# Two layers on one core: the sum of squares of the attention output one weight unit later, and another order behind it on ScalarE and VectorE

## The reference

```python
qkv = xn @ w_qkv                                 # 2048 -> 3 * 2048, weights in fp32
q = rotary(rmsnorm(q, q_g)); k = rotary(rmsnorm(k, k_g))      # 8 heads of 2 x 128
p = softmax(masked(q k^T * scale))               # per head two maps of 256 x 256, in blocks of 128
w = p[:, :, 0] - lam * p[:, :, 1]
o = w @ v                                        # 256 features per head
o = rmsnorm(o, subln_g) * (1.0 - lambda_init)    # over the 256 features of one head
h = h + o.reshape(b, s, 2048) @ w_o
```

## Time and profile before

| | us |
|---|---|
| median of 3 executions | 2826.38 |
| lowest and highest | 2822.13, 2827.9 |
| the profiled execution | 2824.52 |
| its span, first to last instruction | 2822.7 |
| TensorE busy | 2742.0 (97%) |
| VectorE busy | 1984.2 (70%) |
| ScalarE busy | 1192.2 (42%) |
| granted TensorE clock, mean | 0.99 |

### The profile page before, as it was taken

One profiled execution on the slowest core, in us unless ns is written; L12 is line 12 of the kernel. 1 busy time (PEld: TensorE's weight loads), 2 busy tenths in 40 slices (PEclk: granted clock), 3 DMA queues, 4 the chain that ended last, 5 costly groups with the idle time before them and its releaser, 6 DMA issues.

```text
span 2822.7 us, 43966 instructions
## 1 busy us (share of the span) xinstructions
PE 2742.0 (97%) x15236; PEld 2383.8 (84%) x15236; DVE 1984.2 (70%) x2617; ACT 1192.2 (42%) x1517; POOL 5.7 (0%) x12
## 2 busy tenths in 40 slices
PE   6899999999999999999999999999999999999999
PEld 5787888877877888888888888888888888888888
DVE  6555477776767777766777776687777776677765
ACT  2102454444444444444444543355444444444443
POOL 0000000000000000000000000000000000000000
PEclk9999999999999999999999999999999999999999
DMA  9886655544444666666666566654466666666664
GB/s 299 292 259 202 206 188 179 182 142 153 153 131 155 189 192 186 186 191 188 192 187 188 184 200 189 187 162 133 141 193 182 189 193 190 187 192 186 191 199 146
DMA packets 705761, 528.13 MB, mean 187 GB/s; under 512 B 32205, under 2 KB 694543, under 8 KB 705423
## 3 DMA queue, kind: packets, MB, share of 16 engines
q1 hardware_dynamic: 701728, 523.60, 60.6%
q10 hardware_dynamic: 3951, 3.44, 0.4%
HBM read 523.80 MB, written 2.10 MB: 186 GB/s over the span
## 4 chain that ended last, share of the span: by engine, by line
PE 88%; DVE 6%; issue 2%; DMA 2%; ACT 2%; ACTq 1%; SPq 0%; DVEq 0%
PE acc L647 75%; PE acc L727 2%; PE acc L715 2%; PE acc L916 2%; PE turned L727 1%; PE sums L727 1%; DVE wr L1653 1%; DVE pro_ada L1728 1%; DMA aring<-in_w_ada 1%; DMA two_qturn<-two_q 1%; ACT wr L1204 1%; PE sums L655 0%; PE mixed L837 0%; PE sums L1031 0%; ACTq L1235 0%
## 5 line engine op out<-in xcount | busy, mean ns | idle before, releaser
L647 PE MATMUL acc<-xs,wr 128*128 128x512 f32 (+1 forms) x7680 | 1351.1, 337 | 0.2 <-DVE wr L1653 0.2
L647 PEld LDWEIGHTS acc<-xs,wr 128*128 128x128 f32 x7680 | 1174.9, 188 | 163.6 <-issue 3.8
L1653 DVE TENSOR_TENSOR wr<-raw,wr 128x1024 fp32r<-128x1024 f32 x832 | 1002.0, 1222 | 374.6 <-ACT wr L1204 360.7
L1204 ACT ACTIVATE wr<-raw 128x1024 fp32r<-128x1024 f32 x832 | 870.7, 1058 | 799.0 <-PE acc L647 784.7
L647 PE MATMUL acc<-ys,wr 128*128 128x512 f32 (+1 forms) x4352 | 766.2, 338 | 6.5 <-DVE ys L1687 6.5
L647 PEld LDWEIGHTS acc<-ys,wr 128*128 128x128 f32 x4352 | 669.8, 189 | 98.2 <-DVE ys L1687 6.4
L647 PE MATMUL acc<-wr,xs 128*128 128x512 f32 (+1 forms) x1024 | 193.5, 348 | 0.0
L647 PEld LDWEIGHTS acc<-wr,xs 128*128 128x128 f32 x1024 | 163.6, 195 | 24.3 <-issue 0.5
L1546 ACT ACTIVATE ffn_cv<-ffn_cv 128x256 f32<-128x256 f32 x88 | 36.9, 419 | 245.3 <-DVE ffn_cv L2234 245.3
L1664 DVE TENSOR_REDUCE ffn_ug<-acc 128x512 f32<-128x1024 f32 x88 | 107.8, 1225 | 39.6 <-PE acc L647 39.6
L1728 DVE SCALAR_TENSOR_TENSOR pro_ada<-aring,small,pro_ada 128x512 f32<-128x512 f32 (+1 forms) x112 | 92.4, 825 | 31.3 <-DMA aring<-in_w_ada 24.7
(11 more groups left out here) (306 smaller groups left out, 1504.8 us busy)
## 6 DMA issues: line engine op xcount, KB each, us to landing
raw<-in_ffn_w_up SPq DMA_DIRECT2D x704, 256.0 KB
raw<-in_ffn_w_down SPq DMA_DIRECT2D x160, 512.0 KB
raw<-in_a_w_qkv SPq DMA_DIRECT2D x96, 512.0 KB
raw<-in_b_w_kv SPq DMA_DIRECT2D x64, 512.0 KB
aring<-in_w_ada SPq DMA_DIRECT2D x96, 256.0 KB, 6.6
w<-in_w_in SPq DMA_DIRECT2D x48, 512.0 KB
raw<-in_w_ada SPq DMA_DIRECT2D x32, 512.0 KB, 6.1
raw<-in_w_out SPq DMA_DIRECT2D x32, 512.0 KB
```

Source lines behind the costliest of these rows:

```text
L647: mm = pe.matmul(*ops, start=first and ops is wide, stop=last and ops is wide)
L1204: f(wr[:, s, :, 0:256], raw[:, s, :].rearrange("p (k n) -> p k n", k=UK), ACT.Copy)\
L1653: tt(wr[:, s, :, 256:512], raw[:, s, :].rearrange("p (k n) -> p k n", k=UK), wr[:, s, :, 0:256], ALU.subtract).then_inc(T.unit_split[s].se ...
```

## The change

TensorE calls `diff_out_sums` behind unit 3 of the v pair, not behind unit 2. ScalarE issues the exchange DMAs of q behind the first of two units and not behind the second, and those of k ahead of the output's squares and not behind them. VectorE turns k and splits one more unit between the addition of the squares and the wait for their roots, and makes the low half of `ys` (now `diff_out_lo`) behind the evacuation of v. The last head calls the same two functions one behind the other, in the order that it had.

```diff
 in_v (TensorE)
-                        if live and n == 2:
+                        if live and n == 3:
                             diff_out_sums()
 two_heads (ScalarE)
-                    hi(2)
+                    hi(1)
                     turn_copy(qturn, qA, 1)
+                    hi(1)
                     act.wait_ge(*T.acc_read.next())
                     squares_of(S[1], 1)
                     hi(1)
                     root(2 * TOK, HD)
+                    turn_copy(kturn, kA, 2)
+                    T.heads_out.n += 1
                     if live:
                         diff_out_squares()
-                    turn_copy(kturn, kA, 2)
-                    T.heads_out.n += 1
                     hi(2)
 diff_out (VectorE)
-            def diff_out(tiles, turn=None):
+            def diff_out(turn=None):
...
                 tt(sq[0][:, 0, :], sq[0][:, 0, :], sq[0][:, 1, :], ALU.add).then_inc(*T.out_squares.one())
+                if turn:
+                    turn()
+                    split_units(1)
                 dve.wait_ge(*T.rs_ready.next())
                 for d in range(2):
                     w = stt(tmp[0][:, d, :], oA[:, d, :], small[:, 40 + d:41 + d], rs[:, 0, :], ALU.mult, ALU.mult)
                 w.then_inc(*T.split_me.one())
-                if turn:
-                    turn()
+
+            def diff_out_lo(tiles):
                 own(T.split_me)
                 lo(ys[:, tiles, :], tmp[0][:, :, :])
 two_heads (VectorE)
                     if live:
-                        diff_out(slice(0, 2) if first else bass.ds(i * 4 + (2 + 2 * e), 2), lambda: head_turn(kA, kturn))
+                        diff_out(lambda: head_turn(kA, kturn))
                     else:
                         T.sq_ready.n += 2
                         head_turn(kA, kturn)
-                    split_units(1 if live else 2)
+                        split_units(2)
                     evac(vA[:, :, :], by="partitions")
+                    if live:
+                        diff_out_lo(slice(0, 2) if first else bass.ds(i * 4 + (2 + 2 * e), 2))
 behind the loop (VectorE)
-            diff_out(slice(14, 16))
+            diff_out()
+            diff_out_lo(slice(14, 16))
```

## The result

The changed kernel takes 2792.7 us, the median of four executions (2792.3 to 2795.6), against 2827.1 before. The ratio is 0.9883, with a 95% interval of 0.9866 to 0.9900 (the quotient of the two medians, 0.9878, lies in it too). The profiled executions, 2824.52 and 2792.86, are 31.7 us apart where the sum said 25.4. One execution further down, of the kernel with the TensorE edit alone, took 3840.8 us at a granted clock of 0.66; its ratio leaves that one out, and the median without it is 2811.5 in place of 2811.6.

The account below looks back on a forecast made before the run. TensorE, busy 97% of the span, was taken as the bound, so only its pauses or slow stretches could pay. Terms -16.85, -7.6 and -1.0 gave -25.4 us, from 2824.52 to 2799.1, stated as 2800, range 2794 to 2810.

Parts of the forecast that it names:

- the sum: Total saving over the two-heads code and the last head: 25.4 us off the profiled 2824.52 us.
- The wait at L1044: TensorE's idle time before the squares' product, in seven heads, goes: -16.85 us.
- This edit alone takes the whole wait: Issuing product L1044 one unit later on TensorE removes its wait by itself: at least -16.7 us over seven heads.
- the reorderings do not take the wait; they give it a margin: ScalarE's and VectorE's new orders only make the squares' addition ready earlier, 2.1 us ahead of V3's end.
- The clock: Half-clock dips behind five of the seven L1044 pauses vanish with the pauses: -7.6 us, bounds 0 and -10.9.
- rival A: The clock is not given back after the pauses go: gain 17.8 us, 2807.6 us; chance 0.08.
- The last head: Behind the loop, the second scores product's 0.98 us wait for ScalarE's exponentials goes: -1.0 us, bounds 0 and -1.0.
- bare work: Distance between neighbouring L1044 rows less the wait: one head without pause or dip, 39.95 us.
- The walk: Step-by-step timing of the second head under the new order, from the trace of before; product L1044 starts at 615.75.
- B: The stall moves to the scores bank, TensorE waiting 1 us a head: 2814.6 us; chance 0.05.
- C: k's exchange DMAs land late and hold up VectorE's turn of k: slower, 2834 us; chance 0.03.
- D: Nothing changes because the waits at L1044 only stand one unit later: 2826 us; chance 0.03.

Follow-up runs that it names:

- orders-only kernel: The changed kernel with the product L1044 back behind unit 2, so only ScalarE's and VectorE's new orders remain: 2801.0 us, ratio 0.9913.
- five copies: The changed kernel with five 128x512 copies added on VectorE between v's evacuation and the low part of ys, in each of seven heads: 2803.3 us, ratio 0.9925.
- k's DMAs late: The changed kernel with k's exchange DMAs issued behind the roots of the output, about 9 us later: 2825.2 us, ratio 1.0003.

## Why the prediction was right, and where not

*The wait at L1044* (-16.85): right in sum and in place; no idle time in any of the seven heads, and the addition ends some 2 us ahead of the product, as said.

*"This edit alone takes the whole wait"; "the reorderings do not take the wait; they give it a margin"*: the step that failed. I looked at what L1044 waits for and not at who waits for L1044. Moving the product by 2.8 us moves the roots, and in the old order VectorE turned k behind them: 1.1 us a head at the first scores product, in seven heads of seven. The edit alone gives 13.8 us (2825.5 to 2811.6), the whole change 34.4; of the stage, 13.7 and 27.5. VectorE's new order, costed at nothing gained and nothing lost, is worth 10 to 15 us once the product has moved. That the total did not suffer is luck: the edits that were called a margin were made together with the one that needed them. The edits do not add: the two reorderings alone already give 24.4 us (21.0 of the stage), as they cut the pause from 2.4 to 0.7 us, and the dips go with it.

*The clock* (-7.6): right, and rival A fell: no granted clock below 1.00 from 564 to 826.5 us, and no head of 41.5 us. The 22.8 us of the six distances divide into 15.0 us of waits, 6.1 of four dips and 1.6 of restarts (below); this is a division and no test, since the price of a dip and of a restart were read from the same distances. The Trainium skill, TensorE: Matmul & The Clock Gate, "What's actually happening", was on the side of this step: activity releases the throttle. The trace agrees, by the same granted clock.

*The last head* (-1.0): the 0.98 us before its second scores product are gone.

*The sum*: 25.4 forecast for the stretch, 27.5 measured. What is missing is what a pause costs beyond its recorded length. A head was to be 39.95 us; it is 39.68. The 0.27 us a head, 1.9 us for seven, were in my "bare work", because I had only heads with a pause to read it from. (The walk calls a unit of 2.8 us half of a row of 5.85, which is 2.9. The size is right and the reason is not: three units take 8.65 us in a row of the trace of after, 2.80 more than two, so such a row has a tail of 0.25 us.) The further 4.1 us of the profiled pair are the first stage and the late dip. The median of before also stood 2.6 us above its profiled execution, that of after did not.

*Rivals B, C, D*: none came. B's place is the right one, with 1.4 us to spare where I had 1.8. C's mechanism is real: an issue some 9 us later than the kernel's ate the whole gain. No lateness between was tried. D's condition was never near.

## What to carry to other kernels

Before moving a wait, follow both directions: what the waiting instruction waits for, and everything that hangs on its result; in a chain that is written out by hand, the moved step drags the ones behind it. Work that the bounding engine needs soon goes ahead of work that it needs several units later: that order on VectorE was worth 10 to 15 us once the product had moved, and the same remedy 5 us in another stage. And price a pause of TensorE in this kernel at its length, plus 0.3 us, plus 1.3 to 2.9 us of half-clock time, which came behind 17 of the 22 pauses of 1.8 us and more and behind none of up to 1.6 us in the heads.

## What the runs showed that was not expected

A pause costs TensorE about 0.27 us more than the idle time that the profile gives: 39.95 to 39.68 us in the change, 0.7 us of wait for 1.0 us of head in the orders-only kernel, and 0.20 for 0.47 when q's sum was moved. The heads with the five copies show 0.24 to 0.26, and those with k's DMAs late and no dip 0.25 for each of their pauses. The rows of the second head show where it is. First after, without a wait, then before (where L1044 starts at 615.59):

```profile
602.98 8.65 PE L647 MATMUL acc<-wr,xs 128*128 128x512 f32 x48
611.48 0.59 PE L1044 MATMUL sums<-sq,ones 128*128 128x256 f32 x2
611.72 3.13 PE L647 MATMUL acc<-xs,wr 128*128 128x512 f32 x16
```

```profile
615.93 4.70 PE L647 MATMUL acc<-wr,xs 128*128 128x512 f32 x16
```

Without a wait L1044 starts 0.15 us ahead of the end of the row before it (611.63): neighbouring rows overlap, and idle time, which is counted from the end of that row, leaves this part of a pause out. And from the start of L1044 to the next product it is 0.24 us after and 0.34 before, as its row is 0.59 and 0.69 us long. That makes 0.25 of the 0.27 us. The ends of matmuls are modelled, so how the two parts divide is less sure than their sum.
